# Token-major projections of a hybrid mixer in pieces of 512, 512, 512 and 192 columns

## What is computed

```python
proj = h @ w_in          # 256 x 1024 @ 1024 x 3512
ml_q, ml_k, ml_v, ml_o, ml_g, na_q, na_k, na_v, g_q, g_k, g_v, g_g, g_a = split(proj)
# mLSTM heads (6 x 64), forward and backward
ml_out = head_rms_norm(h_f + h_b, ml_norm_g, 6) * sigmoid(ml_o)
# neighbourhood attention (5 heads x 64)
na_out = neighbourhood_attention(na_q, na_k, na_v, na_rpb)
# gated linear attention (5 heads x 64 values), forward and backward
gla_out = head_rms_norm(o_f + o_b, gla_norm_g, 5) * silu(g_g)
return concat(ml_out, na_out, gla_out) @ w_out
```

## Time and profile before

| | before |
|---|---|
| median of 3 runs | 842.92 us (842.56 to 843.38) |
| profiled execution, its own time | 842.58 us |
| its span | 840.8 us |
| TensorE matmul busy | 830.2 us, 99% |
| TensorE weight load busy | 773.4 us, 92% |
| VectorE busy | 612.3 us, 73% |
| ScalarE busy | 493.7 us, 59% |
| granted TensorE clock | 0.998 |
| DMA | 151.40 MB, mean 180 GB/s |

### The profile page before, as it was taken

The page is one execution under the profiler, slowest core; times in us unless marked ns, Lnnn a source line. Parts: engine busy times, 40 slices in busy tenths (PEclk is TensorE's granted clock), DMA queues, the critical chain, the costliest instruction groups (busy, mean ns, idle before and its releaser), DMA issues.

```text
span 840.8 us, 15177 instructions
## 1 busy us (share of the span) xinstructions
PE 830.2 (99%) x6413; PEld 773.4 (92%) x6413; DVE 612.3 (73%) x850; ACT 493.7 (59%) x693; POOL 19.4 (2%) x39
## 2 busy tenths in 40 slices
PE   8999999999999999999999999999999999999997
PEld 7999998889899999999999999888998999999996
DVE  5898977779667566556577988887776776667665
ACT  7955765577665454444568647745765654454534
POOL 5000001000000000000000000010000000000000
PEclk9999999999999999999999999999999999999999
DMA  9777654544437555565446555436516455565551
GB/s 327 239 136 224 228 183 152 200 138 164 150 104 248 200 201 182 178 205 187 151 146 237 151 172 184 179 130 233 175 68 201 149 200 201 186 215 169 182 175 51
DMA packets 112973, 151.40 MB, mean 180 GB/s; under 512 B 3785, under 2 KB 92809, under 8 KB 112905
## 3 DMA queue, kind: packets, MB, share of 16 engines
q1 hardware_dynamic: 112760, 150.16, 53.5%
q10 hardware_dynamic: 144, 0.26, 0.1%
HBM read 147.92 MB, written 1.18 MB: 177 GB/s over the span
## 4 chain that ended last, share of the span: by engine, by line
PE 96%; DVE 1%; ACT 1%; DMA 1%; issue 0%; SPq 0%; ACTq 0%
PE bank L755 26%; PE bank L756 25%; PE bank L757 25%; PE bank L837 5%; PE bank L880 3%; PE bank L964 2%; PE bank L1166 1%; PE bank L1144 1%; PE bank L902 1%; PE bank L977 1%; DMA raw<-in_w_few 1%; PE bank L821 1%; PE bank L1151 0%; PE bank L1099 0%; PE bank L1114 0%; PE bank L1012 0%
## 5 line engine op out<-in xcount | busy, mean ns | idle before, releaser
L1647 DVE TENSOR_TENSOR wlo<-raw,whi 128x2048 fp32r<-128x2048 f32 (+3 forms) x140 | 298.6, 2138 | 96.2 <-ACT whi L1256 95.2
L1256 ACT ACTIVATE whi<-raw 128x2048 fp32r<-128x2048 f32 (+3 forms) x144 | 257.2, 1789 | 49.9 <-PE bank L757 39.2
L755 PE MATMUL bank<-yhi,whi 128*128 128x256 f32 x688 | 190.6, 277 | 0.0
L756 PE MATMUL bank<-ylo,whi 128*128 128x256 f32 x688 | 190.3, 277 | 0.0
L757 PE MATMUL bank<-yhi,wlo 128*128 128x256 f32 x688 | 190.3, 277 | 0.0
L756 PEld LDWEIGHTS bank<-ylo,whi 128*128 128x128 f32 x688 | 129.4, 188 | 0.8
L755 PEld LDWEIGHTS bank<-yhi,whi 128*128 128x128 f32 x688 | 129.2, 188 | 0.9
L757 PEld LDWEIGHTS bank<-yhi,wlo 128*128 128x128 f32 x688 | 129.2, 188 | 0.0
L755 PE MATMUL bank<-whi,xhi 128*128 128x512 f32 (+2 forms) x256 | 90.2, 352 | 0.3 <-issue 0.3
L757 PE MATMUL bank<-whi,xlo 128*128 128x512 f32 (+2 forms) x256 | 88.5, 346 | 0.0
L756 PE MATMUL bank<-wlo,xhi 128*128 128x512 f32 (+2 forms) x256 | 88.4, 346 | 0.0
(11 more groups left out here) (317 smaller groups left out, 1389.1 us busy)
## 6 DMA issues: line engine op xcount, KB each, us to landing
raw<-in_w_up SPq DMA_DIRECT2D x44, 1024.0 KB, 5.0
raw<-in_w_down SPq DMA_DIRECT2D x22, 1024.0 KB, 4.8
raw<-in_w_in SPq DMA_DIRECT2D x10, 1024.0 KB, 5.0
raw<-in_w_xk SPq DMA_DIRECT2D x8, 1024.0 KB, 5.4
raw<-in_w_xv SPq DMA_DIRECT2D x8, 1024.0 KB, 4.9
raw<-in_w_out SPq DMA_DIRECT2D x8, 1024.0 KB, 5.0
raw<-in_w_xq SPq DMA_DIRECT2D x8, 1024.0 KB, 5.2
raw<-in_w_xo SPq DMA_DIRECT2D x8, 1024.0 KB, 4.9
```

The lines of the kernel that those rows point to most:

```text
L755: mm(o, s_hi, m_hi, start=first, stop=False, skip_group_check=True)
L756: mm(o, s_hi, m_lo, start=False, stop=False, skip_group_check=True)
L1256: A(weight(whi, gu), raw[:, gu % RING, 0:SIZE[gu]], ACT.Copy).then_inc(hi_done, 1)
L1647: tt(weight(wlo, gu), raw[:, gu % RING, 0:SIZE[gu]], weight(whi, gu), ALU.subtract).then_inc(lo_done, 1)
```

## The change

The 1728 token-major columns are cut anew: `v` has the 384 columns of `ml_v` and the first 128 of `ml_o`; `gg` has the last 192 columns of `g_g`; `nv` has `na_v` and the next 192 of `ml_o`; `gv` has the last 64 of `ml_o`, `g_v`, and the first 128 of `g_g`. Unit `o` is gone. `gg` runs right after `gk` in step 2 of the mLSTM loop; steps 3, 4 and 5 have one half each (`nva`, `nvb`, `gva`), and `gvb` stands in step 0 of the neighbourhood loop. Two of the units have two ranges of columns, so each of their halves is loaded by two DMAs. The decay rows go out before the load of `gga`, which is now the unit after `gk`. On VectorE `heads_sum` is parted into `heads_divided` (now at three places) and `directions_added`, and `decayed` stands in step 2 of the neighbourhood loop. The core of the diff:

```diff
+        tm_of(name, m, halves, (c, n))
+
+    def tm_of(name, m, halves, *columns):
         for half in halves:
-            u.append(((l, name + half), m, 4 * "ab".index(half), 4, ((c, n),)))
+            u.append(((l, name + half), m, 4 * "ab".index(half), 4, columns))
...
-    tm("v", "w_in", C_V, ML)
+    tm("v", "w_in", C_V, 512)
     fm("nq", "w_in", (C_NQ, 256))
     fm("nk", "w_in", (C_NK, 256))
     fm("gk", "w_in", (C_GK, P))
-    tm("nv", "w_in", C_NV, NA)
-    tm("gv", "w_in", C_GV, GV)
-    tm("o", "w_in", C_O, ML)
-    tm("gg", "w_in", C_GG, GV)
+    tm("gg", "w_in", C_GG + P, 192)
+    tm_of("nv", "w_in", "ab", (C_NV, NA), (C_O + P, 192))
+    tm_of("gv", "w_in", "ab", (C_O + 320, 64), (C_GV, GV + P))
...
-ML_FILL = (("nq",), ("nk",), ("gk",), ("nv0", "nv1"), ("gv0", "gv1"), ("o0", "o1"))
-WIDTH = {"v": ML, "nv": NA, "gv": GV, "o": ML, "gg": GV}
+ML_FILL = ("nq", "nk", "gk", "nva", "nvb", "gva")
...
-                if name == "nva":
+                if name == "gga":
                     sp.wait_ge(scan_ready, l + 1)
                     sp.dma_start(a["rows"][l], gA[:, :]).then_inc(rows_out, 16)
...
-                if name == "gva" and l == 0:
+                if name == "nva" and l == 0:
...
-                if name == ("xk2" if l else "xk0") and UNITS[gu - 1][0] == (l, "ggb"):
+                if gu > 1 and UNITS[gu - 2][0] == (l, "gvb"):
...
+                def fill(unit):
+                    if unit[-1] in "ab":
+                        tm_half(unit[:-1], unit[-1], (unit[:-1] + "0", unit[:-1] + "1"), 512, "n1")
...
+                    if hh == 2:
+                        tm_unit("gg", ("gg0", "gg1"), 192, "n1")
...
                     if hh == 0:
-                        tm_unit("gg", ("gg0", "gg1"), GV, "n1")
+                        tm_half("gv", "b", ("gv0", "gv1"), 512, "n1")
...
-                    elif nm[0] == "o":
-                        drain(A(eo[:, int(nm[-1]), :], b[:, 0:ML], ACT.Tanh, scale=0.5))
+                    elif nm[:2] == "nv":
+                        t = int(nm[-1])
+                        A(nav[:, t, :], b[:, 0:NA], ACT.Copy)
+                        drain(A(eo[:, t, P:320], b[:, NA:512], ACT.Tanh, scale=0.5))
                     elif nm[:2] == "gg":
                         t = int(nm[-1])
-                        A(gg[:, t, :], b[:, 0:GV], ACT.Copy)
-                        drain(A(eg[:, t, :], b[:, 0:GV], ACT.Tanh, scale=0.5))
+                        A(gg[:, t, P:GV], b[:, 0:192], ACT.Copy)
+                        drain(A(eg[:, t, P:GV], b[:, 0:192], ACT.Tanh, scale=0.5))
                     else:
-                        drain(A((nav if nm[:2] == "nv" else gv)[:, int(nm[-1]), :], b[:, 0:GV], ACT.Copy))
+                        t = int(nm[-1])
+                        A(eo[:, t, 320:ML], b[:, 0:64], ACT.Tanh, scale=0.5)
+                        A(gv[:, t, :], b[:, 64:64 + GV], ACT.Copy)
+                        A(gg[:, t, 0:P], b[:, 384:512], ACT.Copy)
+                        drain(A(eg[:, t, 0:P], b[:, 384:512], ACT.Tanh, scale=0.5))
...
+                    A(mv[:, t, :, 0:DH], bank(f"v{t}")[:, 0:ML].rearrange("p (h d) -> p h d", d=DH), ACT.Copy)
+                    drain(A(eo[:, t, 0:P], bank(f"v{t}")[:, ML:512], ACT.Tanh, scale=0.5))
...
-                ahead = (("gk",), ("nva",), ("nvb",), ("gva", "gvb"), ("oa", "ob"), ("gga", "ggb"))
+                ahead = ("gk", "gga", "ggb", "nvb", "gva", "gvb")
...
+                        if hh == 3:
+                            take("gg0")
+                            take("gg1")
+                        split_hi(ahead[hh])
+                        if hh == 0:
+                            silu_tanh(2)
+                        if hh == MLH - 1:
+                            act.wait_ge(bc_ready, l + 1)
+                            is_drained(act, l, f"mls{hh}")
+                            A(b1[:], zc, ACT.Exp, scale=1.0 / 16).then_inc(eb_ready, 1)
+                            A(b3[:], zc, ACT.Exp, scale=-1.0 / 16).then_inc(eb_ready, 1)
+                        if hh < 3:
+                            take(ML_FILL[hh])
+                        if hh == 2:
+                            split_hi("nva")
+                        if hh == 4:
+                            take("nv0")
+                            take("nv1")
...
-                def heads_sum(a, b):
+                def heads_divided(a, b):
...
+                def directions_added(a, b):
                     link(tt(mlh[:, :, a:b, :], hraw[:, :, 0, a:b, 0:DH], hraw[:, :, 1, a:b, 0:DH], ALU.add))
-                ahead = ("nk", "gk", "nvb", "gva", "oa", "gga")
-                between = {4: "gvb", 5: "ob"}
+                ahead = ("nk", "gga", "ggb", "nvb", "gva", "gvb")
...
-                    if hh in between:
-                        split_lo(between[hh])
+                    if hh == MLH - 1:
+                        heads_divided(0, 3)
...
+                        split_lo("nva")
+                heads_divided(3, MLH - 1)
+                directions_added(0, MLH - 1)
...
-                        heads_sum(MLH - 1, MLH)
+                        heads_divided(MLH - 1, MLH)
+                        directions_added(MLH - 1, MLH)
                         split_lo("xk2" if l else "xk0")
...
                     if hh == 2:
                         for g in NA_PAIRS[1]:
                             shares_of(g)
+                        decayed()
                         if l:
                             half_lo("xk3", 1)
                         tails()
```

More of the change, by code:

```diff
@@ L154, in layer_events @@
             job(f"mls{h + 1}", 1)
-        if h < MLH and len(ML_FILL[h]) == 1:
-            job(ML_FILL[h][0], (7, 6)[h % 2], ML_FILL[h][0])
-        elif h < MLH:
-            tm(ML_FILL[h][0][:-1], (7, 6))
+        if h < 3:
+            job(ML_FILL[h], (7, 6)[h % 2], ML_FILL[h])
+            if h == 2:
+                tm("gg", (6, 3))
+        elif h < MLH and h != 4:
+            used(ML_FILL[h])
+        elif h == 4:
+            job("nv0", 7)
+            job("nv1", 6, "nvb")
     for h in range(NAH + 2):
@@ L168, in layer_events @@
         if h == 0:
-            tm("gg", (7, 6))
+            job("gv0", 7)
+            job("gv1", 6, "gvb")
         for i in NA_FILL[l][h]:
@@ L237, in layer_drains @@
             s.append(f"mlo{h - 1}")
-        if h < MLH:
-            s += ML_FILL[h]
+        if h < 3:
+            s.append(ML_FILL[h])
+        elif h < 5:
+            s += [["gg0", "gg1"], ["nv0", "nv1"]][h - 3]
     for h in range(NAH + 2):
@@ L243, in layer_drains @@
         if h == 0:
-            s += ["gg0", "gg1"]
+            s += ["gv0", "gv1"]
         s += [f"xk{i // 2}" for i in NA_FILL[l][h] if i % 2]
@@ L634, in _ @@
                         sp.dma_start(decay_row(hh), bass.AP(v.tensor, v.offset, [[0, P], [32 * T, 2], [1, T]])).then_inc(rows_in[hh], 16)
-                if name == "nva" and l == 0:
+                if name == "gga" and l == 0:
                     sp.wait_ge(memroot_ready, TT)
@@ L643, in _ @@
                     sp.dma_start(memT[:], a["mem_by_features"].rearrange("(k p) t -> p k t", p=P)).then_inc(memT_in, 16)
-                if name == "gva" and l + 1 < DEPTH:
+                if name == "nva" and l + 1 < DEPTH:
                     is_filled(sp, l, "z11")
@@ L886, in tm_unit @@
                         tm_half(unit, half, names, n, group, fresh)
-                def fill(names):
-                    if len(names) == 2:
-                        tm_unit(names[0][:-1], names, WIDTH[names[0][:-1]], "n1")
+                def fill(unit):
+                    if unit[-1] in "ab":
+                        tm_half(unit[:-1], unit[-1], (unit[:-1] + "0", unit[:-1] + "1"), 512, "n1")
                     else:
-                        fm_unit(names[0], "n1")
+                        fm_unit(unit, "n1")
                 def turn_tokens(group, t, src=tmb):
@@ L1406, in _ @@
                     if hh < MLH:
-                        for i, nm in enumerate(ML_FILL[hh]):
-                            if i < len(ahead[hh]):
-                                split_hi(ahead[hh][i])
-                            if hh == 0:
-                                silu_tanh(2)
-                            if hh == MLH - 1 and i == 0:
-                                act.wait_ge(bc_ready, l + 1)
-                                is_drained(act, l, f"mls{hh}")
-                                A(b1[:], zc, ACT.Exp, scale=1.0 / 16).then_inc(eb_ready, 1)
-                                A(b3[:], zc, ACT.Exp, scale=-1.0 / 16).then_inc(eb_ready, 1)
-                            take(nm)
+                        if hh == 3:
[16 more added lines that the diff above has]
+                            take("nv1")
                 split_hi("xk2" if l else "xk0")
@@ L1441, in _ @@
                         memory_hi("mem", l, range(4))
-                        take("gg0")
-                        is_used(act, l, "ggb")
+                        take("gv0")
```

(9 more changed lines are left out.)

5 lines of the change are left out of this document (2 added, 3 removed).

## The result

The changed kernel takes 857.1 us (median of 4 runs, 855.5 to 859.1) against 842.7 before: the ratio is 1.017, with a 95% interval of 1.0157 to 1.0182. It is slower, as forecast, but by 14.4 us and not by 3.7, far outside the range of 843.4 to 849.0. The profiled execution took 857.59 us with a span of 855.8 us, 15.0 more than the span before.

A forecast was written before the change was run, and what follows sets the result against it. TensorE, busy for 99% of the span, was taken as the bound. Terms 0.6 - 0.4 + 1.7 + 1.5 + 0.3 = +3.7 us on 842.58, with the median 0.34 above, gave 846.5 us, range 843.4 to 849.0.

The forecast's parts named there:

- Part 1: TensorE's stream, same columns in other pieces: 192-column matmuls at 112 ns, 512-column at 227.0 ns; +0.6 us in all.
- B: Rival: 192-column matmuls follow the line to 92 ns, no stall comes, 841.2 us; chance 0.07 together with C.
- C: Rival: uniform price per matmul, so 96 fewer are a small gain, 842.7 us; chance 0.07 together with B.
- A: Rival: the stalls do not come, VectorE finds the cover after all, 843.1 us; chance 0.12.
- Part 2: Wait before head 2's outputs goes, as the 192-column unit stands ahead of them: -0.4 us for two layers.
- Part 3: Less cover before the first neighbourhood transposes: 0.65 us stall per layer, 0.4 us for late VectorE in layer 0; +1.7 us.
- Part 4: decayed moved ahead of xk3's second half-split stalls layer 1's xk3: +1.5 us, bounds 0.8 and 2.3; layer 0 nothing.
- Part 5: The rest: last head's shares and GLA transposes wait, +0.3 us; SP's queue order, DMAs and ScalarE's extra activations nothing.
- Rival D: A train of late wide halves in the mLSTM stretch, 3.2 us on top, 849.7 us; chance 0.09.

The follow-up runs named there:

- E10: Changed kernel with its loads sent before nvb, 14 tiny matmuls at the start, and the last head's division behind the next weight split: 850.2 us.
- E8: Kernel before with only decayed moved, behind the shares of heads 2 and 3: 846.4 us (1.0041).
- E3: Changed kernel with the next layer's memory rows, memory operand and gate loads sent before nvb instead of nva: 854.1 us (1.0126).
- E2: Kernel before with 16 tiny matmuls (64 instructions) at the start: 849.2 us (1.0062).
- E9: Changed kernel with only 4 tiny matmuls (16 instructions) ahead of keep_clock at the start: 852.9 us, one run.
- E1: Changed kernel with 24 tiny matmuls behind keep_clock at the start: 852.0 us (1.0101).
- E4: Changed kernel with the second half of xk3's low part made before decayed in layer 1: 857.2 us (1.0161).
- E6: Changed kernel with loads sent before nvb, tiny matmuls at the start, and columns cut as 512, 384, 512 and 320: 850.6 us (1.0084).
- E16: E14 with columns cut as 512, 384, 512 and 320, and the next layer's gate loads sent before gva: 845.4 us (1.0023).
- E13: Changed kernel; in layer 1 SP waits for the last matmul of L1083 before loading wo0a: 852.7 us (1.0113).
- E5: Changed kernel with the loads sent before nvb and 24 tiny matmuls at the start: 849.1 us (1.0067).
- E14: Changed kernel with loads before nvb, 14 spread tiny matmuls, layer 1's xk3 half first and squares late, layer 0's division late: 843.9 us (1.0004).

## Why the prediction was wrong

The direction, slower, was right, and the waits that it named came; the size was a quarter of what came, because two mechanisms and one price stood at nothing in the sum: what SP sends ahead of nva (2.7 us), the arrival of TensorE's own program (5.0 us), and the lower clock behind a long stop (1.6 us, twice). The prediction's own sum gives 846.6 us (842.58 + 3.7 + 0.34), of which it says 846.5.

- **Part 1 was right.** The 192-column matmuls came (70.00 - 67.98) / 18 = 112 ns apart, for which I had taken 112, and the 512-column ones 227. Rivals B and C fall, and A with the waits of parts 3 and 4.
- **Part 2 was right**, 0.2 us a layer.
- **Part 3 was short by 1 us**: 1.6 and 1.2 us instead of 1.7 for both. The place, the row and the releaser were the right ones (L1707 at 107.91 and 533.71). E10 shows the chain to be what was said: 1.2 us taken from it takes away the waits of layer 0. In layer 0, VectorE's row maxima started 1.5 us after the scores instead of 0.8, 0.7 us late, for which it had taken 0.4.
- **Part 4 was right** on the wait: 1.6 us in place of 1.5, and 2.25 in E8, alone, for which it gave up to 2.3. Its "nothing there" for layer 0 held too.
- **Part 5's +0.3 us did not come**: the wait of the GLA transposes is 0.2 us before and after.
- **The step that failed first is part 5's "nothing"**, in its sentence on SP's queue: "The decay rows, memory rows and gate loads stay at the same two places of the queue (before the unit after gk, and two units later): nothing." I counted places in the queue and not time. The two units between are now of 192 columns and each half takes TensorE 2.7 us, so the unit behind the loads is wanted sooner, and it is a 1 MB unit that stands behind another 1 MB. The wait was 2.7 us, and E3, which puts the loads one unit later, removes it.
- **The lower clock** was in no term: 1.6 us after each of the two longest stops, about 3 in all, more in this sum than part 3 or part 4. The prediction priced a wait at its length.
- **TensorE's program** was in no term either: 1.3 us in layer 0, 3.7 in layer 1 before the clock. "96 fewer matmuls" came up only as a gain, in rival C. The removed instructions moved the ends of the program's pieces into the small matmuls, as E2 and E9 show. What the trace before had of it was one unexplained stop of 0.3 us behind the small matmuls of layer 1 ("issue", at 548.92 us, which the prediction's "one recorded wait" passed over) and the queue of 51 packets in the page; I read neither.
- **Rival D**, late wide halves, stayed out of the trace of the changed kernel behind nva, but the same pieces had a wait for gva of 1.0 us in layer 0 in E1, E4 and E9, and those of E6 and E16 one of 1.5: the step of five-odd us is near what VectorE and ScalarE need. It is a small part of D.

The sum by measurement: 0.6 - 0.4 + 2.8 + 1.6 for parts 1 to 4, 2.7 + 1.6 for nva and the clock behind it, 1.3 + 3.7 + 1.6 for the program's pieces and the clock, less the 0.3 that the kernel before had there, less 0.3 at the start and 0.1 more in small steps: 15.0 us, as the span has it.

## What to carry to other kernels

Adding or removing instructions on an engine that runs hundreds of tiny ones in a row can cost or give several us far away, since it shifts where the pieces of its program end; look for "issue" stops inside a loop of equal instructions and for the instruction queue's packets beside them, and shift by a few cheap instructions before judging any other edit. When units become shorter, go through the transfer queue in time and not in places: what a queue sends in front of the next unit must fit into the shorter one. A stop of a TensorE that is otherwise always busy can be paid twice: those of 2.5 and 3.7 us were each followed by 3.4 us at half the clock. The total of one run proves little in such a kernel: E1 came near its forecast although two of its terms had moved by 4 us in opposite directions, and E4 equalled the changed kernel with other waits. Compare the stretch that the edit is about.

## What was not expected of the hardware

- TensorE's program comes in packets of 16384 bytes over the same DMA engines as the weights. Its stop was 1.1 and 1.5 us with the way clear or nearly so (E9 in layer 0, E13) and 3.65 to 4.0 us with a 1 MB load in front (the changed kernel, E2). The one stop of the kernel before without a releaser, 0.3 us after the same load, may be of this kind; E2's trace no longer has it.
- Small matmuls of one row group, one behind the other on the same place in PSUM, took 3.01 us for 48 behind `keep_clock`, 63 ns each (E5), and 3.24 us for 28 ahead of it, 116 ns (E10); at that place, over four row groups and banks, 28 took 1.12 us, 40 ns (E14); in the GLA part 1.21 us for 80, 15 ns. Whether the row groups or the banks did it was not tried.
- The 1.2 GHz stretch was 3.4 us long in the changed kernel, both times, and began 1.3 and 0.9 us after TensorE had resumed; in E4 and E8 it was 6.8 us. A wait of 2.00 us was followed by one (E13), one of 2.61 us was not (E9), none of 1.7 us or shorter after the start was. In E1 and E6 one of 3.4 us lies in the start. What decides between them the runs do not show.
